# Expert rows of a routed mixture: weighted when they leave PSUM and added by indirect transfers onto a table of sums by token

## The chip, the cores and the metric

The kernel runs on one core of a Trainium2 chip. The metric is device time in microseconds (us) for one execution, as the median of several runs. All arithmetic is float32.

## The reference

One step of a hybrid decoder layer for 1,024 prompt tokens and 32 sample tokens (1,056 rows of 1,024 numbers). Three token mixers run side by side on a normalised input, their outputs pass one output projection, and the result is added to the input. Then each row is normalised again and goes through a hierarchical mixture of experts, and a last norm ends the step. The part that matters here:

```
def hier_moe(h, p):
    gl = h @ router_group_w + router_group_b          # 4 groups
    gsel = argmax(gl); gw = softmax(gl)[gsel]
    el = (h @ router_expert_w + router_expert_b)      # 16 experts, 4 in each group
    top_v, top_i = top_k(el[gsel], 2)
    tw = softmax(top_v) * gw
    gate = sum over the two choices of one_hot(gsel * 4 + top_i, 16) * tw
    for e in range(16):                               # SwiGLU of width 512
        he = silu(h @ w_gate[e]) * (h @ w_up[e])
        y = y + gate[e] * (he @ w_down[e])
    return y

x = x + mix                                           # residual after the mixers
x = x + hier_moe(rmsnorm(x, norm_ffn))
y_out = rmsnorm(x, norm_final)
```

## The kernel before, in words

The program is a sequence of blocks. The mixers take the first 830 us or so and are not touched. Three parts are touched.

**The output stage** (`output_stage`, from L1532). It projects the mixers' outputs tile by tile (nine tiles of 128 tokens, the last with 32), keeps the residual rows `x` in SBUF in `xy` (the tile "residual"), norms them and stores the normed rows in DRAM as `h2_rows` (L1621; the trace calls it h_rows). Between these stores the SyncE queue (SP) also stores zeros over the whole DRAM table `y_rows` (L1628; "expert_rows"), 5 transfers of 2,560 KB. At its end VectorE computes the routing (L2150 to L2237): the two experts of each token, their weights (`route.w`), and a packing of all (token, choice) pairs into slots. A slot is 32 rows of one expert; there are at most 96. `Bcol` is the one-hot of a pair's slot, `Arow` the one-hot of its place in the slot times an id, and 72 matmuls `Arow x Bcol` (L1925) give, for each slot, the ids of its 32 rows (`route.token`, "slot_rows"). The id is that of a quarter row: a row of 1,024 numbers is four quarters of 256, and a slot lies on the 128 partitions as 4 quarters by 32 rows. Places that no pair fills have the ids of the quarters of row 0. `route.slot` holds, the other way round, the place of each (token, choice) in `y_rows`.

**The experts** (`experts`, L2273). Every engine loops over the slots, q = 0, 1, ...; the loops over experts take their bounds from registers. In this run there are 74 slots, and GpSimd (POOL) and ScalarE (ACT), which loop in rounds of four slots, go through 76. For one slot:

- POOL waits until the gather of slot q has landed and until TensorE (PE) has read the previous slot, copies the ids of slot q + 3 (L2342) and the gathered rows (L2343, to `xg`, "slot_quarters"), drains, and issues the gather of slot q + 3 (L2329): 128 rows of 1 KB. Four buffers rotate.
- PE does the gate and up products of slot q (L2366), the down product of slot q - 1 (L2377), the transposes of slot q + 2 (L2359) and the transpose of the hidden rows of slot q (L2382).
- ACT applies silu (L2422), copies the finished rows out of PSUM into one of four buffers `y` ("slot_out", L2427), and stores them in order in `y_rows` (L2429), one row for each (token, choice).
- SP loads the weights of expert e + 3 as soon as PE has done with those of expert e: three buffers, 6 MB for an expert (gate and up at L2250 or L2266, down at L2270).

**The end** (`combine`, L2461). For each tile of tokens POOL gathers, from `y_rows`, the row of the first choice and the row of the second (L2478, 18 gathers of 512 KB, the last two of 128 KB). VectorE (DVE) multiplies each by its weight and adds it to the residual (L2509). ACT sums squares (L2497) and gets the scale with Ln and Exp (L2499, L2501), DVE scales by it and by norm_final (L2521), and SP stores the tile (L2487). Three pairs of buffers rotate.

## Time and profile before

| | us |
|---|---|
| median of 3 runs (1550.14 to 1559.4) | 1551.28 |
| the profiled execution, whole | 1556.24 |
| its span in the trace | 1554.5 |

| stretch of the span | us |
|---|---|
| output stage | about 835 to 1036 |
| experts | about 1036 to 1504 |
| end | about 1504 to 1554.5 |

The span is 1.74 us shorter than the profiled execution's own time, and that execution is 4.96 us longer than the median. In the tables of stretches a column gives how long each engine was busy; "PEclk" is the TensorE clock granted, as a share of full speed; "DMA share" is the mean busy share of the core's 16 DMA engines and GB/s what they moved. In rows of the timeline the first number is the start in us, the second how long the row lasted (or, for several instructions merged in one row, the time from the first to the last), and in brackets stands how long the engine was idle before and what ended it. "issue" is time in which the engine waited for nothing that the trace names.

### The profile page before, as it was taken

How to read it: one execution, taken by the hardware profiler on the slowest of the kernel's cores; microseconds unless marked ns; L12 is line 12 of the kernel's file. 1: busy time of each engine (PE TensorE's matmuls, PEld its weight loads, DVE VectorE, ACT ScalarE, POOL GpSimd, SP SyncE). 2: the span in 40 equal slices, each digit the busy share in tenths (PEclk: the TensorE clock that was granted, in tenths of full speed). 3: DMA queues.
4: the chain of work that ended last, by engine and by line, in shares of the span. 5: the costliest groups of instructions: out<-in, count | busy, mean ns of one | idle time of the engine just before them, and what ended most of it. 6: DMA issues, size and time to landing. Idle time of an engine off the chain costs nothing. (4 is left out here: it accounts for less than half of the span.)

```text
span 1554.5 us, 36931 instructions
## 1 busy us (share of the span) xinstructions
PE 1389.8 (89%) x15811; PEld 924.7 (59%) x15812; DVE 442.5 (28%) x1014; ACT 350.0 (23%) x823; POOL 362.4 (23%) x623
## 2 busy tenths in 40 slices
PE   7999999799999999999996999929999999999840
PEld 6666666466656988888883554425555555555520
DVE  3035533222222344444442112041111111111117
ACT  4012111232343233333321221200111111111113
POOL 8000000000003455455523021012222222222223
PEclk9999999899999799999998999959999999999985
DMA  5111111111101000000017434294555556999737
GB/s 170 27 42 37 33 41 27 27 28 41 28 19 28 2 9 9 9 9 9 9 52 251 172 155 149 66 357 165 203 209 206 201 215 215 332 375 317 262 124 260
DMA packets 118505, 190.12 MB, mean 122 GB/s; under 512 B 14496, under 2 KB 63127, under 8 KB 118410
## 3 DMA queue, kind: packets, MB, share of 16 engines
q1 hardware_dynamic: 100792, 159.30, 29.4%
q0 software_dynamic: 7392, 19.26, 3.7%
q10 hardware_dynamic: 10226, 10.19, 2.0%
q8 instruction: 73, 1.20, 0.3%
q14 instruction: 22, 0.18, 0.0%
HBM read 153.79 MB, written 34.92 MB: 121 GB/s over the span
## 5 line engine op out<-in xcount | busy, mean ns | idle before, releaser
L354 PE MATMUL ps<-hT,w_in 128*128 128x352 f32 (+1 forms) x1296 | 396.6, 465 | 0.8 <-DVE conv_state_T L702 0.8
L354 PEld LDWEIGHTS ps<-hT,w_in 128*128 128x128 f32 x1296 | 247.1, 191 | 140.5 <-issue 4.5
L2329 POOL DMA_INDIRECT gathered<-h_rows,gather_rows x79 | 76.4, 967 | 175.9 <-issue 167.7
L2366 PE MATMUL ps<-qkv,slot_T 128*32 128x256 f32 x1920 | 112.5, 387 | 4.3 <-issue 3.2
L2448 DVE TENSOR_TENSOR slot_T<-ps,vecs 128x256 f32<-128x256 f32 x75 | 31.8, 425 | 282.9 <-PE ps L2366 271.2
L2422 ACT ACTIVATE slot_silu<-ps 128x128 f32<-128x128 f32 x77 | 21.3, 277 | 307.0 <-PE ps L2366 299.1
L2366 PEld LDWEIGHTS ps<-qkv,slot_T 128*32 128x32 f32 x1920 | 60.7, 111 | 47.3 <-issue 11.5
L2366 PE MATMUL ps<-cb,slot_T 128*32 128x256 f32 x1408 | 80.5, 380 | 5.6 <-issue 5.6
L326 POOL DMA_DIRECT2D out_gdn_conv_prompt<-vbn x1 | 0.5, 518 | 297.2 <-ACT vbn L637 297.2
L1699 PE MATMUL ps<-qkv,zg 128*128 128x512 f32 (+1 forms) x144 | 66.2, 602 | 0.0
L2366 PEld LDWEIGHTS ps<-cb,slot_T 128*32 128x32 f32 x1408 | 43.9, 110 | 35.7 <-issue 9.6
L2377 PE MATMUL ps<-qkv,slot_hidden_T 128*32 128x256 f32 x960 | 57.4, 379 | 0.4 <-DVE slot_hidden_T L2458 0.4
L2427 ACT ACTIVATE slot_out<-ps 128x256 f32<-128x256 f32 x76 | 29.1, 383 | 104.6 <-PE ps L2377 104.6
L2458 DVE COPY slot_hidden_T<-ps 128x128 f32<-128x128 f32 x74 | 21.6, 292 | 108.1 <-PE ps L2382 108.1
L2342 POOL COPY gather_rows<-slot_rows 128x1 uint32 x76 | 14.3, 188 | 162.7 <-PE ps L2359 160.5
L778 DVE SCALAR_TENSOR_TENSOR zg<-pre,vecs,zg 128x1024 f32<-128x1024 f32 x36 | 46.2, 1284 | 3.5 <-issue 1.0
L2028 DVE TENSOR_TENSOR residual<-residual,ps 128x512 f32<-128x512 f32 (+1 forms) x18 | 12.3, 686 | 115.9 <-PE ps L1699 115.9
L2359 PE MATMUL ps<-ident,slot_quarters 128*128 128x128 f32 x152 | 33.5, 302 | 12.8 <-POOL slot_quarters L2343 12.8
L2377 PEld LDWEIGHTS ps<-qkv,slot_hidden_T 128*32 128x32 f32 x960 | 31.6, 110 | 20.6 <-issue 0.6
L1699 PEld LDWEIGHTS ps<-qkv,zg 128*128 128x128 f32 (+1 forms) x144 | 24.7, 181 | 30.1 <-issue 29.5
L2377 PE MATMUL ps<-third_w_down,slot_hidden_T 128*32 128x256 f32 x704 | 42.0, 379 | 0.0
L2377 PE MATMUL ps<-zg,slot_hidden_T 128*32 128x256 f32 x704 | 42.0, 379 | 0.0
(601 smaller groups left out, 2235.7 us busy)
## 6 DMA issues: line engine op xcount, KB each, us to landing
w_in<-in_w_in SPq DMA_DIRECT2D x28, 512.0 KB, 4.0
expert_rows<-zero_rows SPq DMA_DIRECT2D x5, 2560.0 KB, 9.4
qkv<-in_expert_w_gate SPq DMA_DIRECT2D x6, 2048.0 KB
qkv<-in_expert_w_up SPq DMA_DIRECT2D x6, 2048.0 KB
qkv<-in_expert_w_down SPq DMA_DIRECT2D x6, 2048.0 KB, 16.4
cb<-in_expert_w_gate SPq DMA_DIRECT2D x5, 2048.0 KB, 9.7
cb<-in_expert_w_up SPq DMA_DIRECT2D x5, 2048.0 KB, 16.7
zg<-in_expert_w_down SPq DMA_DIRECT2D x5, 2048.0 KB
```

Source lines behind the costliest of these rows:

```text
L354: last = pe.matmul(pbank(b)[:, c, 0:n], w[:, k, :], hT[:, k, c * CH:c * CH + n], start=(k == 0), stop=(k == KD - 1))
L778: dve.scalar_tensor_tensor(a_p, x_p, wv, a_p, ALU.mult, ALU.add)
L1699: last = pe.matmul(ps[0:n, half, :], mix[k][:, where(i)], wo[:, k, half * 512:half * 512 + 512], start=(k == 0), stop=(k == KD - 1))
L2329: pool.indirect_dma_start(ring[r][:], None, quarter_rows, bass.IndirectOffsetOnAxis(ap=idx[:, r:r + 1], axis=0)).then_inc(in_ring[r], 16)
L2342: pool.tensor_copy(idx[:, ahead:ahead + 1], route.token[:, ds(q + RING - 1, 1)])
L2359: last = pe.transpose(xT_bank[:, a * P:a * P + P], xg[:, a * P:a * P + P], m.ident[:])
L2366: last = pe.matmul(gu_bank[c4[c], 0:2 * QF].rearrange("p (x f) -> p x f", x=2), xT[:, k % 2, k // 2, :], by_block[u][k][:, :, c * QF:c * Q ...
L2377: last = pe.matmul(y_bank[c4[c], 0:QD], heT[:, c4[k]], wd[u][:, k, c * QD:c * QD + QD], start=(k == 0), stop=(k == 3))
L2422: act.activation(sl[:], gu_bank[:, 0:QF], ACT.Silu).then_inc(s.silu, 1)
L2427: act.activation(y[r][:], y_bank[:, 0:QD], ACT.Copy).then_inc(s.acc, 1)
L2448: dve.tensor_tensor(xT[:], xT_bank[:, 0:2 * P].rearrange("p (s c t) -> p s c t", s=2, c=4), bc(nf, 3, ROWS_SLOT), ALU.mult).then_inc(s.xT, 1)
L2458: dve.tensor_copy(heT[:], hT_bank[:, 0:QF]).then_inc(s.hT, 1)
```

## The change

- Two DRAM tables get 32 spare rows. `y_rows`, its zeros and `route.slot` go. Instead SP stores each residual tile in a table `sum_rows` right after the store of its normed rows, and zeros in the spare rows of both tables.
- Places of a slot that no pair fills now have the ids of spare rows, each its own, so that the 128 ids of a slot all differ. For this the ids are computed as an offset from the spare rows (a few more DVE operations at the start of the output stage, `behind`).
- A second product of 72 matmuls, at the start of the expert block, gives the weight of each place of each slot (`route.weight`); `Arow` is multiplied by the choice weights for it. DVE copies it out before the first slot.
- ACT scales a slot's rows by these weights when it copies them out of PSUM, and no longer issues a store.
- POOL issues, one slot after the other, an indirect transfer that adds the 128 quarter rows onto `sum_rows`. Before each it waits until the previous one has landed (`out_y[(r - 1) % RING]`), since two slots may hold the same token. The gather comes without a drain now. In the loop POOL does `next_rows(q + 4)` (the old work, for slot q + 4) and then `add_rows(q)`.
- The end loads the nine tiles of `sum_rows` in order on SP, ACT does the sums of squares (Ln and Exp once for two tiles), DVE one scaling, and SP stores.

```diff
@@ output_stage, SP @@
                 def out_rows(i):
                     sp.wait_ge(s.h2, i + 1)
                     sp.dma_start(h2_rows[where(i), :], h2[i % 2][0:rows(i), :]).then_inc((s.h2o0, s.h2o1)[i % 2], 16)
-
-                blank = y_rows.rearrange("(z p a) d -> z p a d", z=5, p=P)
+                    sp.dma_start(sum_rows[where(i), :], x_tile(i)).then_inc(s.xo, 16)
+
                 for i in range(6):
                     out_rows(i)
-                    if i < 5:
+                    if i == 0:
                         sp.wait_ge(s.zeros, 1)
-                        sp.dma_start(blank[i], bc(zeros[:], 1, ROUNDS * RING * ROWS_SLOT // (5 * P))).then_inc(s.zf, 16)
+                        for spare_of in (h2_rows, sum_rows):
+                            sp.dma_start(spare_of[NTOK:NTOK + ROWS_SLOT, :], xy[NS:2 * NS, NT, :]).then_inc(s.xo, 16)
@@ output_stage, DVE, routing @@
                 for c, w in enumerate((w1, w2)):
-                    dve.tensor_copy(route.w[:, c, :], w[:].rearrange("p t o -> p (t o)"))
+                    dve.tensor_copy(route.w[:, c, 0:NT], w[:, 0:NT, 0])
+                    dve.tensor_tensor(route.w[:, c, NT:TILES], w[:, NT, :], valid[:], ALU.mult)
...
                 for c in range(2):
-                    last = dve.tensor_tensor(by_choice[:, c], by_choice[:, c], bc(ids[:], 2, ROWS_SLOT), ALU.mult)
+                    last = dve.tensor_tensor(by_id[:, c], by_choice[:, c], behind[:], ALU.mult)
                 last.then_inc(s.rt, 1)
-
-                dve.scalar_tensor_tensor(rk[:], fk[:], float(ROWS_SLOT), rk[:], ALU.mult, ALU.add)
+                dve.drain()
+                for c in range(2):
+                    dve.tensor_tensor(by_choice[:, c], by_choice[:, c], bc(route.w[:, c, :], 2, ROWS_SLOT), ALU.mult)
@@ experts, POOL @@
-                pool.tensor_copy(idx[:, 0:RING - 1], route.token[:, 0:RING - 1])
+                def next_rows(q, r, loads, copies):
+
+                    pool.wait_ge(in_ring[r], 16 * loads)
+                    pool.wait_ge(s.xTp, q + 1)
+                    if copies is not None:
+                        pool.wait_ge(s.xg, q)
+                        pool.wait_ge(s.ix, copies)
+                    pool.tensor_copy(idx[:, r:r + 1], route.token[:, ds(q + RING, 1)]).then_inc(s.ix, 1)
+                    pool.tensor_copy(xg[:], ring[r][:]).then_inc(s.xg, 1)
+                    gather((r + RING - 1) % RING)
+
+                def add_rows(q, r, stored, copies):
+
+                    pool.wait_ge(s.acc, q + 2)
+                    if stored is not None:
+                        pool.wait_ge(out_y[(r - 1) % RING], 16 * stored)
+                    pool.wait_ge(s.ix, copies)
+                    pool.tensor_copy(sidx[:, (r + 1) % RING:(r + 1) % RING + 1], route.token[:, ds(q + 1, 1)]).then_inc(s.ix, 1)
+                    pool.indirect_dma_start(quarter_sums, bass.IndirectOffsetOnAxis(ap=sidx[:, r:r + 1], axis=0), y[r][:], None,
+                                            compute_op=ALU.add).then_inc(out_y[r], 16)
...
-                n = rounds(pool)
-                with pool.Fori(0, n) as i:
+                m = more_rounds(pool)
+                for r in range(RING):
+                    next_rows(r, r, 1, r if r else None)
+                for r in range(RING):
+                    next_rows(r + RING, r, 2, RING + 2 * r)
+                    add_rows(r, r, 1 if r else None, RING + 2 * r + 1)
+                with pool.Fori(1, m) as i:
                     for r in range(RING):
-                        q, ahead = RING * i + r, (r + RING - 1) % RING
-                        pool.wait_ge(in_ring[r], 16 * (i + 1))
-                        pool.wait_ge(s.xTp, q + 1)
-                        pool.tensor_copy(idx[:, ahead:ahead + 1], route.token[:, ds(q + RING - 1, 1)])
-                        pool.tensor_copy(xg[:], ring[r][:]).then_inc(s.xg, 1)
-                        pool.drain()
-                        gather(ahead)
+                        q = RING * i + r
+                        next_rows(q + RING, r, i + 2, RING + 2 * q)
+                        add_rows(q, r, i + 1 if r else i, RING + 2 * q + 1)
+                for r in range(RING):
+                    q = RING * m + r
+                    add_rows(q, r, m + 1 if r else m, RING + 2 * RING * m + r)
@@ experts, PE @@
+                for a in range(2 * TILES):
+                    for c in range(4):
+                        last = pe.matmul(ps[c4[c], 7, 0:TABLE], row_weights[:, a, :], slot_onehot[:, a, :], start=(a == 0), stop=(a == 2 * TILES - 1))
+                last.then_inc(s.wt, 1)
@@ experts, ACT @@
-                    act.activation(y[r][:], y_bank[:, 0:QD], ACT.Copy).then_inc(s.acc, 1)
-                    act.wait_ge(s.acc, q + 2)
-                    act.dma_start(y_rows[ds(q * ROWS_SLOT, ROWS_SLOT), :].rearrange("t (c f) -> c t f", c=4), y[r][:]).then_inc(out_y[r], 16)
+                    act.activation(y[r][:], y_bank[:, 0:QD], ACT.Copy, scale=route.weight[:, ds(q, 1)]).then_inc(s.acc, 1)
@@ combine, SP @@
-                sp.dma_start(wrow, A["norm_final"].partition_broadcast(P)).then_inc(s.w, 16)
+                for t in range(TILES):
+                    sp.dma_start(x[t][0:n[t]], sum_rows[t * P:t * P + n[t], :]).then_inc(x_in[t], 16)
+                    if t == 1:
+                        sp.dma_start(wrow, A["norm_final"].partition_broadcast(P)).then_inc(s.w, 16)
```

On POOL, one slot of the expert loop (the last of a round of four) stood so before; "gathered" are the four ring buffers, "slot_quarters" is `xg`, and the rows ISA are waits.

```order
L2342 ISA
L2342 COPY gather_rows<-slot_rows 128x1
L2343 COPY slot_quarters<-gathered 128x256
L2329 DMA gathered<-h_rows,gather_rows 128x256
L2337 REGISTER_ALU
L2337 COMPARE_AND_BRANCH
```

The same slot now:

```order
L2359 ISA
L2360 ISA
L2360 COPY gather_rows<-slot_rows 128x1
L2361 COPY slot_quarters<-gathered 128x256
L2350 DMA gathered<-h_rows,gather_rows 128x256
L2369 REGISTER_ALU
L2370 ISA
L2370 COPY scatter_rows<-slot_rows 128x1
L2371 DMA sum_rows<-slot_out,scatter_rows 4352x256
L2385 REGISTER_ALU
L2385 COMPARE_AND_BRANCH
```

The adding transfer (L2371) and its copy of ids now stand on POOL behind the gather of each slot, with waits ahead of the copy. The store of a slot has left ACT's queue.

On SP, from the end of the expert block to the end of the program, there stood:

```order
L2294 UNCONDITIONAL_BRANCH
L2481 UNCONDITIONAL_BRANCH
L2483 DMA qkv<-in_norm_final 128x1024
L2487 DMA out_y_prompt<-residual 128x1024 x8
L2487 DMA out_y_sample<-residual 32x1024
```

And now:

```order
L2311 UNCONDITIONAL_BRANCH
L2527 UNCONDITIONAL_BRANCH
L2530 DMA qkv<-sum_rows 128x1024 x2
L2532 DMA qkv<-in_norm_final 128x1024
L2530 DMA qkv<-sum_rows 128x1024 x6
L2530 DMA qkv<-sum_rows 32x1024
L2536 DMA out_y_prompt<-qkv 128x1024 x8
L2536 DMA out_y_sample<-qkv 32x1024
```

Nine loads now stand ahead of the nine stores on the same queue, and the 18 gathers on POOL are gone.

## Rows read from the trace of the kernel before

**Rows 1.** Stretches: us, busy time of each engine with instructions, clock, DMA share, GB/s.

```profile
1020.00:1035.00 15.00, 5.65 (x144) 5.30 (x148) 8.69 (x30) 0.00 (x0) 0.00 (x0) 0.55 1.04 392
...
1200.00:1300.00 100.00, 98.06 (x1675) 56.51 (x1671) 15.35 (x51) 11.02 (x34) 26.22 (x52) 1.00 0.56 204
...
1440.00:1460.00 20.00, 17.89 (x309) 10.26 (x305) 2.73 (x9) 1.98 (x6) 3.91 (x9) 1.00 1.03 382
1475.00:1500.00 25.00, 21.06 (x356) 11.96 (x348) 3.46 (x12) 3.91 (x14) 5.43 (x10) 1.00 0.17 51
1520.00:1540.00 20.00, 0.00 (x0) 0.00 (x0) 16.84 (x14) 6.91 (x17) 11.33 (x9) 0.50 0.99 364
```

**Rows 2.** Timeline of PE: the gate and up products of two slots in a row.

```profile
1190.28 3.66 PE L2366 MATMUL ps<-qkv,slot_T 128*32 128x256 f32 x64
...
1196.07 3.66 PE L2366 MATMUL ps<-qkv,slot_T 128*32 128x256 f32 x64
```

**Rows 3.** Waits of PE in the expert stage: us in total, times, longest.

```profile
PE ps L2359 <- POOL slot_quarters L2343: 12.8, 8, 8.0
```

**Rows 4.** Timeline of POOL, gathers back to back and then with PE as the slower.

```profile
1068.13 0.97 POOL L2329 DMA_INDIRECT gathered<-h_rows,gather_rows  x1 [2.08 <-issue]
...
1069.23 0.40 POOL L2343 COPY slot_quarters<-gathered 128x256 f32<-128x256 f32 x1
1071.65 0.97 POOL L2329 DMA_INDIRECT gathered<-h_rows,gather_rows  x1 [2.02 <-issue]
...
1220.81 0.96 POOL L2329 DMA_INDIRECT gathered<-h_rows,gather_rows  x1 [0.84 <-issue]
```

**Rows 5.** The same: first and last of 12 gathers issued with POOL never free.

```profile
1398.90 0.97 POOL L2329 DMA_INDIRECT gathered<-h_rows,gather_rows  x1 [5.10 <-issue]
...
1473.32 0.97 POOL L2329 DMA_INDIRECT gathered<-h_rows,gather_rows  x1 [4.44 <-issue]
```

**Rows 6.** The gather's line over the whole span: landing, counted from the issue's start.

```profile
DMA to landing us min/median/max: 2.7/5.4/7.2
```

**Rows 7.** Timeline of PE: first slots of two experts with three slots each.

```profile
1411.64 3.66 PE L2366 MATMUL ps<-qkv,slot_T 128*32 128x256 f32 x64 [0.48 <-issue]
1430.85 3.66 PE L2366 MATMUL ps<-cb,slot_T 128*32 128x256 f32 x64 [1.75 <-issue]
```

**Rows 8.** DMA issues by line: KB each, median us to landing.

```profile
qkv<-in_expert_w_gate SPq DMA_DIRECT2D x6, 2048.0 KB
...
out_y_sample<-residual SPq DMA_DIRECT2D x1, 128.0 KB, 2.0
```

**Rows 9.** Timeline of the routing, the second product's model, and of the first gather.

```profile
1018.42 0.24 DVE L2188 COPY choice_weights<-r_w 128x9 f32<-128x9 f32 x2
...
1029.63 0.82 DVE L2225 TENSOR_TENSOR ub<-ub,quarter_rows 128x288 f32<-128x288 f32 x2 [0.43 <-issue]
...
1030.51 4.80 PE L1925 MATMUL ps<-bb,ub 128*32 128x104 f32 x144 [9.35 <-DVE ub L2225]
...
1037.06 1.11 POOL L2329 DMA_INDIRECT gathered<-h_rows,gather_rows  x1 [0.88 <-issue]
...
1042.74 0.18 POOL L2342 COPY gather_rows<-slot_rows 128x1 uint32 x1 [2.05 <-DMA gathered<-h_rows,gather_rows]
```

**Rows 10.** Timeline of the end: last evictions and stores, first and last instructions.

```profile
1496.97 0.38 ACT L2427 ACTIVATE slot_out<-ps 128x256 f32<-128x256 f32 x1
...
1500.28 0.55 ACTq L2429 DMA_DIRECT2D expert_rows<-slot_out  x1
1504.21 0.34 SPq L2483 DMA_DIRECT2D qkv<-in_norm_final  x1
...
1552.13 0.34 SPq L2487 DMA_DIRECT2D out_y_sample<-residual  x1
```

**Rows 11.** Queues and groups of the end alone (1504 to 1554.5): packets, MB, share.

```profile
q0 software_dynamic: 2400, 8.65, 49.4%
q1 hardware_dynamic: 1344, 4.85, 25.2%
```

More of the change, by code:

```diff
@@ L58 @@
 gb gcum kd gl gcT gcs gco bk zt zte""".split()
-MOE_SEMS = "g0 g1 g2 d0 d1 d2 r0 r1 r2 r3 ix xg xTp xT gu silu he hTp hT down acc y0 y1 y2 y3".split()
-FIN_SEMS = "w c0 c1 c2 used rstd y out".split()
+MOE_SEMS = "g0 g1 g2 d0 d1 d2 r0 r1 r2 r3 wt wtd ix xg xTp xT gu silu he hTp hT down acc y0 y1 y2 y3".split()
+FIN_SEMS = "w x0 x1 x2 x3 x4 x5 x6 x7 x8 ones rstd y out".split()
 ROWS_SLOT, SLOTS, RING = 32, 96, 4
@@ L2492, in _ @@
                 act.preload_act_table_set(LNEXP)
-                for t in range(TILES):
-                    n = P if t < NT else NS
-                    act.drain()
-                    act.wait_ge(s.used, t + 1)
-                    act.activation(junk[0:n], xy[0:n, t, :], ACT.Square, accum_out=ssq[0:n, t, 0:1])
-                    act.drain()
-                    act.activation(ssq[0:n, t, 1:2], ssq[0:n, t, 0:1], ACT.Ln, scale=1.0 / D, bias=NORM_EPS)
-                    act.drain()
-                    act.activation(ssq[0:n, t, 0:1], ssq[0:n, t, 1:2], ACT.Exp, scale=-0.5).then_inc(s.rstd, 1)
+                act.wait_ge(s.ones, 1)
@@ new lines, in _ @@
+                for a, b in groups:
+                    for t in range(a, b):
+                        act.wait_ge(x_in[t], 16)
+                        act.activation(junk[0:n[t]], x[t][0:n[t]], ACT.Square, accum_out=ssq[0:n[t], 0, t:t + 1])
+                        act.drain()
+                    act.activation(ssq[:, 1, a:b], ssq[:, 0, a:b], ACT.Ln, scale=1.0 / D, bias=NORM_EPS)
+                    act.drain()
+                    act.activation(ssq[:, 0, a:b], ssq[:, 1, a:b], ACT.Exp, scale=-0.5).then_inc(s.rstd, 1)
@@ L2503, in _ @@
             @block.vector
             def _(dve):
-                def add(t):
-                    n = P if t < NT else NS
-                    dve.wait_ge(got[t % 3], 32 * (t // 3 + 1))
-                    for c in range(2):
-                        last = dve.scalar_tensor_tensor(xy[0:n, t, :], rows[t % 3][c][0:n], route.w[0:n, c, t:t + 1], xy[0:n, t, :], ALU.mult, ALU.add)
-                        if c == 0:
-                            dve.drain()
-                    last.then_inc(s.used, 1)
+                dve.memset(ssq[:], 1.0).then_inc(s.ones, 1)
```

127 lines of the change are left out of this document (69 added, 58 removed).

## The prediction

> **What bounds the kernel now.** I read the stretches first, then the timelines of PE and POOL in the expert stage, then the timeline of the end. From 1100 to 1475 PE is busy almost throughout; between 1200 and 1300 it is 98.06 of 100 us [rows 1]. One slot takes 1196.07 - 1190.28 = 5.79 us of PE [rows 2], and 74 of them are 428 of the stage's 468 us, which also hold its first gathers and its last stores. So the expert stage is bound by PE, and a term that lengthens POOL's work costs nothing until POOL needs more than 5.79 us for a slot.
>
> POOL is near that point. A gather lands 2.7 us after its issue starts at best, 5.4 in the median and 7.2 at worst [rows 6]. Where POOL is behind, the next gather starts 1071.65 - 1068.13 = 3.52 us after the last, and the copies between them end 2.0 us before it; where PE is the slower, the gap ahead of the gather is 0.84 [rows 4]. 2.7 + 0.84 = 3.54: I read this as the drain, which holds POOL until the previous gather has landed. Under heavy weight traffic the same distance is (1473.32 - 1398.90) / 11 = 6.77 us [rows 5], so a gather lands there in 6.77 - 0.84 = 5.9 us. This is over 5.79: in that stretch POOL sets the pace, and PE waits for its copies; over the whole stage these waits are 12.8 us in 8 places, 8.0 of them before the first slot [rows 3].
>
> From 1497.35, when the last real slot has been evicted, to 1554.5 is a tail of 57.2 us [rows 10]. In it the DMA engines are the bound: 0.99 busy at 364 GB/s from 1520 to 1540 [rows 1], with 8.65 MB gathered and 4.85 MB on the other queue (norm_final and the stores) [rows 11].
>
> **Part 1, the output stage.** The zeros (5 x 2,560 KB) go and 4.3 MB of residual rows come; both lie beside 150 us of PE work, and no PE wait names them: 0. The routing chain at its end is exposed. The weights take four instructions for two: +0.2 (two last 0.24 [rows 9]). The multiplication that forms the ids keeps its size. Multiplying `Arow` by the weights costs 0.8 us (as L2225, 0.82) and lies beside the 4.8 us of the first product [rows 9]. Sum +0.3; bounds 0 and +1.5. The second product is another 4.8 us of PE, from about 1036.3; the first gathered rows are there only at 1042.74 [rows 9], so it is covered with over a microsecond to spare, and 0 is taken; without that cover it would cost at most 4.8.
>
> **Part 2, the expert stage.** Removed: the store on ACT, which nothing waits for, and the drain on POOL. Its best gain is what PE waits for POOL after the first slot, 12.8 - 8.0 = 4.8 us. Added: one indirect transfer for each slot, in a chain. Each waits for the one before to land, then comes a copy of ids (0.19) and a gap like those before an issue (0.3) and the semaphore (about 0.15): period = landing + 0.65. Behind the waiting transfer stands the work for the next slot's rows, and PE waits for that.
>
> The landing of a transfer that adds onto DRAM is in no row. The nearest is the gather, the same 128 rows of 1 KB on the same queue. Quiet, I take 3.5 us (2.7, and 0.8 for a read of the table ahead of the write); its period is then 4.15, under 5.79, and free. Under load the low bound is the gather's 5.9. The high bound is 9.1: the gather's loaded part, 5.9 - 2.7 = 3.2, paid twice. I take 7.5, the middle, since the nearest row is 5.9 and there are a read more and a gather just ahead in the same queue. The loaded period is 8.15.
>
> An expert's weights are three times 2,048 KB [rows 8], 6.29 MB, at 375 GB/s (between 364 and 392 [rows 1]) 16.8 us. In the experts of five to eight slots the loaded 16.8 us see two chain steps, which put POOL behind by 2 x (8.15 - 5.79) = 4.7 us; POOL may lag about 5 to 7 us before PE misses its rows (with PE as the slower it copies them most of a slot ahead of their use), and then catches up at 4.15. Cost 0. The experts of three slots are another matter: from 1411.64 to 1430.85 one took 19.2 us [rows 7]. With the chain: 16.8 / 8.15 = 2.06 slots while loaded, 0.94 x 4.15 = 3.9 us for the rest, 20.7 us in all, +1.5. There are seven such from 1357 on: +10.5, less 4.5 of the lag that is allowed and not used up before: **+6**. With 5.9: period 6.55, 2.56 slots, 1.8 us for the rest, 18.6: no loss, and up to 4.8 gained. With 9.1: period 9.75, 1.72 slots, 5.3, 22.1 us: +2.9 x 7 = **+20**.
>
> The Trainium skill has a rule that speaks against this part. "Collectives: The Full Stack", section "The bandwidth ceiling", says of adding in the DMA path that it is slow not for the add but for its two source reads on one ring, and gives a ratio of 1.93 for throughput. No row here shows an adding transfer. By that rule the loaded landing would be at the 9.1 end, a rival below.
>
> **Part 3, the tail.** Before: 57.2 us. Now, from 1497.35: slots 74, 75 and 76 (the last two of them empty) are added in a chain. 0.5 to the first issue, 3 x 3.5 + 2 x 0.65 = 11.8 to the last landing. Before, from the last store's issue at 1500.28 to SP's first instruction at 1504.21 were 3.9 us [rows 10]; with 2.0 for the landing of 128 KB [rows 8], 1.9 are left for the change of blocks. So the end begins at 1497.35 + 0.5 + 11.8 + 1.9 = 1511.6, 7.3 later than before. Its traffic: 4.33 MB of sums and 0.52 MB of norm_final in, 4.33 MB out, 9.2 MB against 13.5, at 375 GB/s 24.5 us, with 1.5 to the first byte and 1.0 after the last: 27. DVE, busy 16.84 of 20 us there with three operations for a tile [rows 1], has one left, and ACT was busy 6.91; both lie beside the transfers. End at 1538.6: **-16**. Bounds: scatters at 2.7 and 392 GB/s give -20, scatters at 6 and 364 give -8.
>
> **Sum.** 0.3 + 6 - 16 = -9.7 on the span: 1544.8, the profiled execution 1546.5, and on the median, which lies 4.96 below that of the profiled execution, 1551.3 - 9.7 = 1541.6. About 1%, some 15.5 us, is what a measurement of this kernel can tell from no change.
>
> **Rivals.**
> - *The adding is as cheap as the gather.* Loaded landing 5.9 and quiet 2.7 to 3. The removed drain speaks for it, and that one queue (ACT's stores) no longer competes. Expert stage -3 to 0, tail -17 to -20: -19, 1532. Against it: there is a read that a gather has not.
> - *Two reads count twice.* Loaded landing 9.1: +20 - 16 + 0.3 = +4, 1555. For it: the stretch from 1399 to 1473 shows POOL already over PE's pace at 5.9. Beside this stands the skill's rule above.
> - *The chain overtakes PE (slower).* The place is the wait before each adding transfer. It decides from a quiet landing of 5.79 - 0.65 = 5.1 us, since then every slot and not only the loaded ones pays. At a quiet landing of 6.0 each of 74 slots costs 0.86 more, 64, less 7 of lag; the tail gives only -8: +49, 1600. At 3.5 quiet and 10.5 loaded (period 11.15: 1.5 slots, 6.2 us, 23 us per expert) it is +27 there and some +8 in the longer experts, so +19, 1570. For it: each step reads, adds and writes DRAM and waits for the receipt, and under load plain gathers take up to 7.2 already [rows 6]. Against it: quiet, 128 KB goes to DRAM in 2.0 us [rows 8], and the gather in 2.7.
>
> **How the numbers follow.** Forecast (landing 6.5 to 8.5 under load, -16 to -2): 0.43, of which 0.12 faster by over 1% and 0.31 within. As cheap as the gather: 0.22, faster. Counted twice: 0.14, within 1%. Chain overtakes PE: 0.21, slower. That is faster 0.34, within 0.45, slower 0.21. The forecast's own range is 1535 to 1550. The range asked for reaches to the cheap case with its best tail, -23 or 1528, and over the two-reads case into the lower half of the slow one, 1578; about 0.1 is left above and 0.07 below.
>
> **What would show it.** The landing of the adding transfer, quiet and loaded: 3.5 and 7.5. POOL's waits before the copy of its ids: none where the DMA share is about 0.5, some between 1350 and 1475. The gap ahead of a gather shrinks to about 0.3 under load. PE's waits for slot_quarters rise from 12.8 to about 20 us. Slots in quiet stretches still take 5.79. Three adding transfers in a row after PE's last product, and then 27 us to the end with DMA at 0.95 or more. I am wrong if quiet slots get longer than 5.79, if SP starts its loads much earlier or later than 14 us after the last real eviction, or if the end block takes far from 27 us.

## The result, and the profile after

| | us |
|---|---|
| before, median of 4 runs (1549.28 to 1559.4) | 1550.71 |
| changed, median of 4 runs (1572.52 to 1575.22) | 1574.06 |
| ratio | 1.0141, 95% interval 1.0107 to 1.0174 |
| span of the profiled execution, before and after | 1554.5 and 1571.8 |

The change makes the kernel slower by 1.4%. 1541.6 was forecast. 1574.06 lies outside the forecast's own range (1535 to 1550) and on the wrong side of no change; it is inside the wider one (1528 to 1578) only because that reaches into the slow rival. One execution of the kernel before, measured beside e10 and e11, took 4,994 us and is left out of their intervals. The spans differ by 17.3 us, and they divide so (each time is the start of an eviction on ACT; before has its first at 1059.02 and the last real one at [rows 10]):

| part | before | after | difference |
|---|---|---|---|
| start of the span to the first eviction | 1059.02 | 1057.36 | -1.7 |
| first to last real eviction, 73 slots on | 437.95 | 467.87 | +29.9 |
| last real eviction to the end | 57.5 | 46.6 | -10.9 |

Two stretches before, and then those of the changed kernel, with the columns of [rows 1]:

```profile
1300.00:1400.00 100.00, 96.11 (x1639) 55.50 (x1635) 15.47 (x51) 11.23 (x34) 23.90 (x49) 1.00 0.87 320
1400.00:1500.00 100.00, 89.02 (x1513) 51.28 (x1505) 13.64 (x45) 11.44 (x36) 22.24 (x45) 1.00 0.66 234
```

```profile
1200.00:1300.00 100.00, 95.19 (x1619) 54.81 (x1612) 14.86 (x49) 12.51 (x33) 55.04 (x84) 1.00 0.66 193
1300.00:1400.00 100.00, 86.94 (x1426) 49.38 (x1422) 12.74 (x42) 10.53 (x28) 46.67 (x70) 0.97 0.91 306
1400.00:1500.00 100.00, 84.31 (x1378) 47.93 (x1374) 12.74 (x42) 10.53 (x28) 50.23 (x77) 0.97 0.76 250
...
1560.00:1570.00 10.00, 0.00 (x0) 0.00 (x0) 5.92 (x5) 3.71 (x10) 0.00 (x0) 0.50 1.00 408
```

Two things stand there. In the stretches with the most weight traffic PE is busy 87 and 84 us of 100, where before it was 96 and 89 (the latter with 3 us after its last eviction); and the granted clock is 0.97 in two stretches in which it was 1.00 before. The clock has two levels, full and half, so a mean of 0.97 over 100 us is 6 us at half clock, and work worth 3 us at full clock is not done in them.

The waits from 1055 to 1500, of POOL and then of PE:

```profile
POOL scatter_rows L2370 <- DMA sum_rows<-slot_out,scatter_rows: 149.4, 61, 5.7
```

```profile
PE ps L2412 <- POOL slot_quarters L2361: 20.7, 16, 2.6
PE ps L2419 <- issue: 15.2, 15, 1.9
```

L2370 is the copy of ids ahead of the adding transfer (L2371), so the first row is the wait for the previous slot's transfer, 61 times for the 69 transfers of this stretch, 149.4 us in all. In the same stretch before, PE waited 3.5 us for POOL's copies and 12.4 on "issue" (the rest of the 12.8 of [rows 3] came ahead of it).

POOL's timeline, two steps under weight traffic and then quiet ones:

```profile
1183.46 1.60 POOL L2371 DMA_INDIRECT sum_rows<-slot_out,scatter_rows  x1 [0.51 <-issue]
1184.49 0.77 POOL L2360 COPY gather_rows<-slot_rows 128x1 uint32 x1
1184.62 0.98 POOL L2361 COPY slot_quarters<-gathered 128x256 f32<-128x256 f32 x1
1185.77 1.01 POOL L2350 DMA_INDIRECT gathered<-h_rows,gather_rows  x1 [0.17 <-issue]
1191.39 0.18 POOL L2370 COPY scatter_rows<-slot_rows 128x1 uint32 x1 [4.61 <-DMA sum_rows<-slot_out,scatter_rows]
1192.08 1.60 POOL L2371 DMA_INDIRECT sum_rows<-slot_out,scatter_rows  x1 [0.50 <-issue]
...
1203.41 1.60 POOL L2371 DMA_INDIRECT sum_rows<-slot_out,scatter_rows  x1 [0.50 <-issue]
...
1207.51 0.18 POOL L2370 COPY scatter_rows<-slot_rows 128x1 uint32 x1 [0.78 <-DMA sum_rows<-slot_out,scatter_rows]
1208.20 1.60 POOL L2371 DMA_INDIRECT sum_rows<-slot_out,scatter_rows  x1 [0.51 <-issue]
```

Read it as a chain. The transfer issued at 1183.46 lets the next copy of ids go at 1191.39: it landed after 7.93 us, and the step to the next issue is 1192.08 - 1183.46 = 8.62 us. Quiet, the landing is 1207.51 - 1203.41 = 4.10 and the step 4.79. A step is the landing and 0.69 us. The issue lasts 1.60 us, where a gather's lasts 0.97 [rows 4], and POOL's copies right behind it last 0.77 and 0.98 instead of 0.18 and 0.40; the gaps ahead of the gathers from 1060 to 1500 are 0.16 to 0.27, so the hold in [rows 5], up to 6.5 us there, is gone with the drain.

What late rows do to PE, two slots of its timeline:

```profile
1374.84 1.91 PE L2430 MATMUL ps<-qkv,slot_hidden_T 128*32 128x256 f32 x32
1378.93 0.43 PE L2412 MATMUL ps<-ident,slot_quarters 128*128 128x128 f32 x2 [2.18 <-POOL slot_quarters L2361]
...
1379.41 5.35 PE L2419 MATMUL ps<-qkv,slot_T 128*32 128x256 f32 x64
...
1387.47 0.43 PE L2412 MATMUL ps<-ident,slot_quarters 128*128 128x128 f32 x2 [0.99 <-POOL slot_quarters L2361]
...
1389.87 5.28 PE L2419 MATMUL ps<-cb,slot_T 128*32 128x256 f32 x64 [1.86 <-issue]
```

The granted clock in two stretches of 5 us inside it (columns: length, PE busy, clock, DMA share, GB/s):

```profile
1380.00:1385.00 5.00, 5.00 (x68) 0.70 1.07 374
...
1390.00:1395.00 5.00, 5.00 (x68) 0.68 1.07 369
```

The waits are paid twice: 2.18 us idle before the transposes at 1378.93, and then a gate and up product of 5.35 us instead of 3.66, because part of it ran at 1.2 GHz. Not every wait has this effect: after those of 2.15 and 2.56 us that ended at 1274.78 and 1312.86 the clock stayed at 1.00.

The end of the stage, in order of time:

```profile
1524.50 1.59 POOL L2371 DMA_INDIRECT sum_rows<-slot_out,scatter_rows  x1 [1.39 <-issue]
...
1525.23 0.47 ACT L2481 ACTIVATE slot_out<-ps,slot_weights 128x256 f32<-128x256 f32 x1
...
1529.25 1.57 POOL L2371 DMA_INDIRECT sum_rows<-slot_out,scatter_rows  x1 [0.47 <-issue]
...
1533.82 1.57 POOL L2371 DMA_INDIRECT sum_rows<-slot_out,scatter_rows  x1 [0.47 <-issue]
1537.91 0.18 POOL L2370 COPY scatter_rows<-slot_rows 128x1 uint32 x1 [2.53 <-DMA sum_rows<-slot_out,scatter_rows]
1538.57 1.57 POOL L2371 DMA_INDIRECT sum_rows<-slot_out,scatter_rows  x1 [0.47 <-issue]
1545.31 0.81 SPq L2530 DMA_DIRECT2D qkv<-sum_rows  x2
```

Four transfers in a row, 4.6 to 4.75 us apart, and SP's first load 19.6 us after the last real eviction has ended. From there to 1571.8 are 26.5 us, where 27 were predicted.

Where the 29.9 us of the stage are: the slots need 432 us when nothing waits (the experiments below). In the changed kernel PE waits 20.7 us for POOL's copies, "issue" is 4.6 more than in e5, which has no such waits (15.2 against 10.6), and PE is busy 10.0 us longer than in e5 (430.7 against 420.7) for the same products: 6 to 7 of these are half clock, and 2 are a stretched down product in the first five and the last slots (below). That is 35.3 of the 35.7 us above 432. Before stood 6 above 432. Of the 20.7 us, 7.2 fall in the long experts ahead of 1357 and 13.5 in the experts of three slots after it.

### The profile page after: what moved, and what is told of

It reads as the page before. It is cut to its first block and busy times, and to the rows that moved or that the text cites. A ratio compares the mean times of both kernels' runs of the same rounds, so it can differ in the third digit from the quotient of the medians.

```text
span 1571.8 us, 37521 instructions
## 1 busy us (share of the span) xinstructions
PE 1402.1 (89%) x15955; PEld 932.1 (59%) x15956; DVE 421.6 (27%) x1006; ACT 355.1 (23%) x815; POOL 480.1 (31%) x757
## 5 line engine op out<-in xcount | busy, mean ns | idle before, releaser
L2371 POOL DMA_INDIRECT sum_rows<-slot_out,scatter_rows x76 | 121.9, 1604 | 36.7 <-issue 28.6
L2419 PEld LDWEIGHTS ps<-qkv,slot_T 128*32 128x32 f32 x1920 | 61.6, 112 | 49.5 <-issue 14.4
L2350 POOL DMA_INDIRECT gathered<-h_rows,gather_rows x79 | 79.7, 1009 | 14.6 <-issue 13.9
L2419 PEld LDWEIGHTS ps<-cb,slot_T 128*32 128x32 f32 x1408 | 45.0, 113 | 38.7 <-issue 14.0
L2370 POOL COPY scatter_rows<-slot_rows 128x1 uint32 (+1 forms) x76 | 14.0, 185 | 159.9 <-DMA sum_rows<-slot_out,scatter_rows 156.8
L2481 ACT ACTIVATE slot_out<-ps,slot_weights 128x256 f32<-128x256 f32 x76 | 36.1, 475 | 114.7 <-PE ps L2430 114.7
L2361 POOL COPY slot_quarters<-gathered 128x256 f32<-128x256 f32 x76 | 61.5, 809 | 0.2 <-issue 0.2
L2360 POOL COPY gather_rows<-slot_rows 128x1 uint32 (+1 forms) x76 | 45.3, 596 | 38.6 <-issue 19.1
L2412 PEld LDWEIGHTS ps<-ident,slot_quarters 128*128 128x128 f32 x152 | 15.4, 141 | 55.3 <-issue 52.3
```

What stands on the lines that cost most here:

```text
L2350: pool.indirect_dma_start(ring[r][:], None, quarter_rows, bass.IndirectOffsetOnAxis(ap=idx[:, r:r + 1], axis=0)).then_inc(in_ring[r], 16)
L2360: pool.tensor_copy(idx[:, r:r + 1], route.token[:, ds(q + RING, 1)]).then_inc(s.ix, 1)
L2361: pool.tensor_copy(xg[:], ring[r][:]).then_inc(s.xg, 1)
L2371: pool.indirect_dma_start(quarter_sums, bass.IndirectOffsetOnAxis(ap=sidx[:, r:r + 1], axis=0), y[r][:], None, compute_op=ALU.add).then_in ...
L2412: last = pe.transpose(xT_bank[:, a * P:a * P + P], xg[:, a * P:a * P + P], m.ident[:])
L2419: last = pe.matmul(gu_bank[c4[c], 0:2 * QF].rearrange("p (x f) -> p x f", x=2), xT[:, k % 2, k // 2, :], by_block[u][k][:, :, c * QF:c * Q ...
```

## The experiments

All but e3 and e9, which start from the kernel before, are edits of the changed kernel; the diffs show the lines that matter. "Stage" is from the first to the last real eviction, "tail" from the start of the latter to the end of the span. Spans and waits are of one profiled execution each; PE's waits are those for POOL's copies of gathered rows in the stage, without what comes ahead of the first eviction. Some kernels leave work out: e4 the adding transfers, e1 the sums (a row holds its last writer's values), e2 and e12 three of the four tables at the end, and e8, e14 and e9 the loads of the weights of experts 3 to 15.

| kernel | time, us | runs | span | stage | PE waits | tail |
|---|---|---|---|---|---|---|
| before | 1550.71 | 4 | 1554.5 | 438.0 | 3.5 | 57.5 |
| changed | 1574.06 | 4 | 1571.8 | 467.9 | 20.7 | 46.6 |
| changed again (e15) | 1576.93 | 1 | 1575.2 | 466.9 | 19.0 | 45.8 |
| no adding transfers (e4) | 1529.56 | 1 | 1527.8 | 430.9 | 0 | 35.2 |
| two tables, wait two back (e5) | 1541.28 | 4 | 1539.4 | 432.2 | 0 | 49.4 |
| the same again (e13) | 1551.7 | 1 | 1550.0 | 432.2 | 0 | 49.5 |
| two tables, wait one back (e11) | 1588.96 | 4 | 1588.7 | 466.8 | 20.4 | 57.1 |
| groups interleaved, wait three back (e6) | 1533.96 | 4 | 1535.5 | 431.6 | 0 | 37.6 |
| groups interleaved, wait one back (e10) | 1577.21 | 4 | 1575.9 | 472.2 | 23.7 | 45.3 |
| plain writes in the chain (e1) | 1555.87 | 1 | 1553.9 | 446.5 | 0.7 | 40.8 |
| four tables (e2) | 1561.29 | 1 | 1558.8 | 453.7 | 0 | 37.6 |
| the same again (e12) | 1537.24 | 1 | 1535.5 | 432.2 | 0 | 37.4 |
| changed, no weight traffic (e8) | 1558.24 | 1 | 1555.6 | 452.4 | 0 | 46.1 |
| the same again (e14) | 1536.66 | 1 | 1534.9 | 431.3 | 0 | 46.1 |
| before, no weight traffic (e9) | 1557.67 | 1 | 1555.9 | 432.7 | 1.6 | 55.3 |
| before without the drain (e3) | 1550.3 | 10 | 1546.7 | 432.4 | 0 | 55.9 |

### The wait alone, with two tables

```
-    pool.indirect_dma_start(quarter_sums, ...
+    pool.indirect_dma_start(tables[r % 2], ...
e5 alone:
-    pool.wait_ge(out_y[(r - 1) % RING], 16 * stored)
+    pool.wait_ge(out_y[(r - 2) % RING], 16 * stored)
```

The second table starts from zeros; the end loads both, and DVE adds them (these edits, the same in e5 and e11, are not shown).

Expected of e5: 

> The changed kernel with two tables (even slots onto the residual rows, odd slots onto zeros), each with its own chain, so a step has two slots' time; the end loads both and adds them. Theory: loaded landing 8.6 + 0.7 is under 2 x 5.79, so the expert stage is back at its old length, 28 us shorter than in the changed kernel, and the adding transfers after the last slot overlap in pairs, 6 to 8 us less; the end has 4.3 MB more to load, 11 us more. Sum -25: about 1548 to 1552 against 1550.7 before and 1574 changed. Rivals A and B: the stage keeps its length and the end is longer: 1580 or more.

Expected of e11: 

> The kernel with two tables of sums (even slots on one, odd slots on the other, both read and added at the end), with the wait for the slot before put back, though the two write to different tables. Theory (the wait is the cost, not two transfers that meet in one table): the expert stage is as long as in the changed kernel (468 us from the first to the last eviction, against 432 with the wait for two back) and the time some 33 to 38 above that of the two tables, 1574 to 1580. Rival (the cost is contention for one table's rows): within 5 us of the kernel with two tables, 1541 to 1546.

Expected of e13, the kernel of e5 beside e11: 

> The kernel with two tables and the wait for two back, once more, beside the four tables on one chip. If the slots of 6.11 us belong to the program of the four tables: 1538 to 1545 with slots at 5.79. If they belong to the chip: as the four tables beside it, plus or minus 5.

e5 takes 1541.28 us, 0.9907 of before (0.9878 to 0.9935), below the 1548 to 1552 that I had expected. e11 takes 1588.96, 1.0221 of the before on its chip (1.017 to 1.0272). The two differ only in which transfer is waited for: the stage goes from 432.2 to 466.8 us and the tail grows by 8. Against e13, on e11's chip, the spans differ by 38.7. The chain is the cost, not two transfers that meet in one table: in e11 neighbours go to different tables and the loss is whole. The time I had expected for e11 (1574 to 1580) was too low because it took e5's run as the base: e13 came out 10 us above e5, with the first eviction at 1068.31 instead of 1057.81 and the same stage. That offset arises ahead of the experts: the routing's product (L1934) starts at 1028.99 in e5 and at 1039.77 in e13. Its cause is open. The times of before spread as widely, from 1547.9 to 1561.6, but whether for the same reason is not shown.

### The order of the experts

e6 takes the experts in the order 0, 4, 8, 12, 1, 5, ... Both experts of a token are of one group, so the two rows of a token then lie at least seven slots apart, and a transfer need only wait for that of three slots back. Each of four neighbouring slots has its own spare rows for empty places. The diff shows the order and the wait; the ids of the spare rows and the unrolled loop on SP are left out.

```
-    sel[:, c].rearrange("p t (g e) -> p t g e", e=EPG)
+    sel[:, c].rearrange("p t (e g) -> p t e g", g=NG)
-    load(3 * i + u, u, bound(sp, 3 * i + u - 2))
+    load((j % NG) * EPG + j // NG, j % 3, bound(sp, j - 2))
e6 alone:
-    pool.wait_ge(out_y[(r - 1) % RING], 16 * stored)
+    pool.wait_ge(out_y[(r - 3) % RING], 16 * stored3)
```

Expected of e6: 

> The changed kernel with the experts in an order in which four neighbours belong to four groups (0, 4, 8, 12, 1, 5, ...). Both experts of a token are of one group and each expert has at least two slots, so slots of one token are at least seven apart; each transfer waits only for the one three slots back. Four sets of spare rows; some 2.5 us more of routing on DVE. One table, the end as in the changed kernel. Theory: expert stage as before or 3 us shorter, adding transfers after the last slot overlap (7 us less), end 26.5 us: 1550.7 - 1.4 + 2.5 - 3 - 18 = about 1531, between 1526 and 1537. Rival A or B: 1560 or more.

Expected of e10: 

> The kernel of the interleaved groups of experts, with the wait of the changed kernel put back: each adding transfer waits for that of the slot before. Same order of the weights, same spare rows, same 76 transfers. Theory (the wait makes POOL late, and what counts is how many steps of the chain fall on weight traffic and whether POOL's lead of 4.6 us is refilled between them): 13 loads of 16.8 us at 8.6 a step are 25 loaded steps, 25 x (8.6 - 5.79) = 71 us of delay, against 49 quiet steps that give back up to 1.0 each: the expert stage comes to 25 x 8.6 + 49 x 4.8 = 450 us at best against 431 of PE alone, and with three steps of tail the time is 1556 to 1572. Rival 1 (the order of the experts brought the gain and the wait costs nothing): 1534, as with the wait for three back. Rival 2 (the order does nothing for the chain): 1574 as the changed kernel.

e6 takes 1533.96 us, 0.9853 of before (0.9816 to 0.9891): the fastest of those that compute everything. It has the same 76 issues of 1.6 us, one table and the end of the changed kernel. PE's only wait for POOL from 1055 to 1500 in e6 ends at 1059.70, ahead of the first eviction at 1066.33:

```profile
PE ps L2430 <- POOL slot_quarters L2379: 0.8, 1, 0.8
```

e10 takes 1577.21, 1.0166 of before (1.0107 to 1.0225), with these waits and, in its first stretches, this clock:

```profile
PE ps L2430 <- POOL slot_quarters L2379: 23.7, 12, 3.6
```

```profile
1100.00:1200.00 100.00, 87.70 (x1413) 49.52 (x1414) 13.02 (x43) 10.89 (x29) 48.57 (x74) 0.95 0.76 250
1200.00:1300.00 100.00, 89.19 (x1477) 50.58 (x1469) 13.56 (x45) 11.26 (x30) 47.16 (x71) 0.97 0.86 287
```

So the order by itself brings nothing, and the second rival of e10 stands. My 450 us for its stage was a best case, in which no quiet step is wasted on a POOL that is already ahead, and it left out the clock, which over e10's stage (0.95, 0.97, 0.98 and 0.97 in four stretches of 100 us) took 13 us. In numbers: 431.6 of e6, 23.7 of waits, 13 of clock and 3.6 more "issue" (13.6 against 10.0) make 471.9, against 472.2 measured.

After the last eviction e6 needs less as well, since its last transfers do not wait for each other:

```profile
1499.29 1.57 POOL L2389 DMA_INDIRECT sum_rows<-slot_out,scatter_rows  x1 [0.27 <-POOL scatter_rows L2388]
...
1501.23 1.57 POOL L2389 DMA_INDIRECT sum_rows<-slot_out,scatter_rows  x1 [0.16 <-POOL scatter_rows L2388]
...
1503.17 1.57 POOL L2389 DMA_INDIRECT sum_rows<-slot_out,scatter_rows  x1 [0.16 <-DMA sum_rows<-slot_out,scatter_rows]
1509.98 0.81 SPq L2548 DMA_DIRECT2D qkv<-sum_rows  x2
```

They are 1.94 us apart instead of 4.6 to 4.75, and the tail is 37.6 us instead of 46.6.

The Trainium skill, "DMA: Bandwidth & Descriptors", section "Rules for kernel authors", has the rule behind the wait: an accumulating DMA reads its destination and writes it later, and nothing holds the bytes in between, so another access of the same bytes must wait for its semaphore. The rule speaks of the same bytes. No run here breaks it, so none shows what that would do. e5 and e6 keep it and are fast; what cost the time was to apply it to neighbouring slots whose bytes could have been kept apart.

### No transfers, plain transfers, four tables

```
e4:  -    pool.indirect_dma_start(quarter_sums, ..., compute_op=ALU.add).then_inc(out_y[r], 16)
     +    pool.sem_inc(out_y[r], 16)
e1:  -    compute_op=ALU.add
e2:  -    pool.wait_ge(out_y[(r - 1) % RING], 16 * stored)
     +    pool.wait_ge(out_y[(r - 3) % RING], 16 * stored3)
     -    pool.indirect_dma_start(quarter_sums, ...
     +    pool.indirect_dma_start(tables[r], ...
```

Expected of e4: 

> The changed kernel without the adding transfers (the experts' results are left out; POOL keeps the waits for the evictions and the copies of ids). It gives the stage with neither chain, nor issues, nor their traffic. Theory: last real eviction 1492 to 1496, and four tables (which has issues and traffic but no chain) within 2 us of this. If four tables is much later than this, the issues or the traffic cost something by themselves.

Expected of e1: 

> The changed kernel, with the transfers to the table of sums as plain writes (no add; so the sums are left out and a row holds its last writer's values). The chain of waits stays. Last real eviction: 1497.35 us before, 1525.70 in the changed kernel. Theory (a chain whose step is the landing of the adding transfer, 4.1 us quiet and 8 to 8.6 under weight traffic, plus 0.7): the read is a part of that landing, so quiet landing about 3 us, loaded about 6, last real eviction near 1500. Rival A (POOL's own instructions, 1.6 us for the issue of an adding transfer, make POOL too slow): the issue falls to about 1.0 us as for the gather, and the eviction comes near 1500 too, but with the landing unchanged. Rival B (the adding transfers take DMA bandwidth from the weights): near 1515, with the landing as it was.

Expected of e2: 

> The changed kernel with four tables of sums, one for each of the four buffers, so that a transfer waits only for the one three slots back; the same 76 adding transfers, each with its read and 1.6 us of issue. The end reads only the first table, so three quarters of the sums are left out. Theory: without the chain the last real eviction is back at 1494 to 1498 (28 us earlier than in the changed kernel), and PE waits for slot_quarters under 5 us. Rival A (POOL's issues): stays at 1520 or later. Rival B (bandwidth): stays at 1515 or later, with PE waiting for weights between 1350 and 1480.

Expected of e12, the kernel of e2 beside e13: 

> The kernel with four tables once more, beside the two tables on one chip. In its first run nothing waited and yet each slot took 6.11 us in place of 5.79: the 32 matmuls of the down product took 2.2 to 2.3 us instead of 1.91. The changed kernel shows the same in its first five and last five slots, where POOL is not late. If this belongs to the program: 1559 to 1562 again, slots at 6.11, while the two tables run at 5.79 beside it. If it belongs to the chip of that batch: both kernels here alike, either 1540 to 1545 or 1562 to 1566.

e4 has the floor: a stage of 430.9 us. e6 does all its transfers in 431.6, e5 and e12 in 432.2. So with the wait out of the way the 1.6 us that POOL spends on each issue and the traffic cost at most 1.3 us together.

e1 keeps the chain but its transfers land sooner. POOL's timeline under weight traffic, and in the tail:

```profile
1423.94 1.01 POOL L2371 DMA_INDIRECT sum_rows<-slot_out,scatter_rows  x1 [0.51 <-issue]
...
1429.90 0.18 POOL L2370 COPY scatter_rows<-slot_rows 128x1 uint32 x1 [3.27 <-DMA sum_rows<-slot_out,scatter_rows]
```

```profile
1514.61 0.98 POOL L2371 DMA_INDIRECT sum_rows<-slot_out,scatter_rows  x1 [0.48 <-issue]
1517.34 0.18 POOL L2370 COPY scatter_rows<-slot_rows 128x1 uint32 x1 [1.75 <-DMA sum_rows<-slot_out,scatter_rows]
```

A plain transfer lands in 5.96 us under traffic and 2.73 quiet, where an adding one takes 7.93 and 4.1; its issue lasts 1.0 instead of 1.6. PE's waits for POOL are 0.7 us, although the wait for the slot before is still there. How much of this the shorter landing does is not shown by itself, since many slots of e1 took 6.11 us (below), which gives the chain more time. The first queue's packets, adding and then plain:

```profile
q0 software_dynamic: 15936, 20.57, 7.0%
```

```profile
q0 software_dynamic: 8640, 20.57, 3.8%
```

7,296 packets more for 76 transfers is 96 more for each, for the same bytes.

The stages of e1, e2 and e8 were nevertheless 16 to 23 us above the floor, with next to no wait in the profile, and the last real evictions came later than I had expected. Nearly all slots of e2 and e8, and many of e1, took about 6.11 us and not 5.79; e1's down products change between 1.91 and 2.2 to 2.3 us within the one execution. The down product of one slot on PE, in e2 and then in e12, a later run of the same kernel:

```profile
1207.91 2.21 PE L2434 MATMUL ps<-qkv,slot_hidden_T 128*32 128x256 f32 x32
```

```profile
1205.35 1.91 PE L2434 MATMUL ps<-qkv,slot_hidden_T 128*32 128x256 f32 x32
```

At a granted clock of 1.00 in both, these 32 matmuls last 2.2 to 2.3 us in nearly all slots of e2, and 1.91 in all of e12. e12 ran at 1537.24 with a stage of 432.2, 24 us under e2. So the stretched product belongs to an execution, or to part of one, and not to the program (the first case of my expectation for e12 falls; the second too, as e9 and e2 shared a chip and only e2 had it). All four executions that show it carry these indirect writes: e1, e2, e8 and, in its first five and last slots only, the profiled one of the changed kernel; but most executions with such writes do not show it. What causes it stays open.

### Without the weight traffic

```
-    load_gate_up(...), load_down(...)        of experts 3 to 15
+    sp.sem_inc(in_gu[u], 16 * loads_gu[u])
+    sp.sem_inc(in_d[u], 16)
```

Expected of e8, on the changed kernel: 

> The changed kernel without the weight loads of experts 3 to 15 (their arithmetic runs on the weights of experts 0 to 2; the loads are left out). Theory: all landings are quiet, a step of the chain takes 4.7 to 4.8 us, under the 5.79 of PE, and the last real eviction comes within 3 us of that of the old kernel treated in the same way. Rival A (POOL's issues): it comes about 25 us later than there. Rival B: within 3 us too.

Expected of e9, the same edit on before: 

> The kernel before without the weight loads of experts 3 to 15 (left out in the same way). It is the measure for the changed kernel so treated. Gathers land in 2.7 us throughout, slots take 5.79 us, so from the first slot (1044.4) 74 slots and 16 starts of experts at about 0.5: last real eviction near 1483 to 1490. All theories.

Expected of e14, the kernel of e8 again: 

> The changed kernel without the weight loads of experts 3 to 15 (their results are computed with the weights of the first three), once more. Theory (the chain costs nothing where its step of 4.1 + 0.7 us is under the 5.79 us of a slot, the whole loss comes from steps under weight traffic): slots at 5.79 unless the down product is stretched again, no wait of PE for POOL's copies, 432 us from the first to the last real eviction, and 46 from there to the end with its four transfers in a row: a time of 1537 to 1548. Rival (POOL's own longer work, 1.6 us to issue an adding transfer beside 1.0 for a gather, costs too): over 440 us in the stage, with waits of PE for POOL's copies.

Expected of e15, the changed kernel beside e14: 

> The changed kernel itself, beside the one without weight traffic on one chip. By the theory 465 to 470 us from the first to the last real eviction, of which some 20 us are PE's waits for POOL's copies and 5 to 15 are half-clock stretches that follow them, and a time of 1570 to 1590. The rival gives the two kernels of this batch the same stage within 5 us.

e8 alone could not be read, for its slots of 6.11 us. e9 says that before hardly depends on the traffic: its stage is 432.7 us against 438.0 (its time is no lower because its first eviction came at 1067.94, with the late start seen above). e14 can be read. Two steps of the chain on POOL, in e14:

```profile
1201.26 1.61 POOL L2375 DMA_INDIRECT sum_rows<-slot_out,scatter_rows  x1 [0.16 <-issue]
1204.90 0.18 POOL L2364 COPY gather_rows<-slot_rows 128x1 uint32 x1 [2.03 <-PE ps L2416]
...
1206.98 1.61 POOL L2375 DMA_INDIRECT sum_rows<-slot_out,scatter_rows  x1 [0.17 <-issue]
```

Here the chain of 4.8 us runs inside a slot of 5.79, and it is POOL that waits for PE. The stage is 431.3 us, with no wait of PE for POOL and a clock of 1.00 to the last product. e15 on the same chip has 466.9, 19.0 us of such waits, and these stretches:

```profile
1200.00:1300.00 100.00, 95.72 (x1608) 54.83 (x1604) 14.54 (x48) 12.03 (x32) 56.76 (x85) 0.98 0.60 177
1300.00:1400.00 100.00, 87.13 (x1442) 49.82 (x1438) 13.15 (x44) 10.80 (x29) 46.74 (x70) 0.97 0.92 310
1400.00:1500.00 100.00, 86.84 (x1374) 48.40 (x1369) 12.31 (x42) 10.25 (x27) 47.71 (x73) 0.93 0.80 260
```

Means of 0.98, 0.97 and 0.93 are 12 us lost to half clock. 19.0 + 12 + 5.1 more "issue" (14.8 against 9.7) is 36.1, for a difference of 35.5. The whole loss of the stage comes from steps of the chain under weight traffic. The tails of e14 and e15 are the same (46.1 and 45.8): there the chain costs its four steps with or without weights.

### Before without the drain

The second experiment on the kernel before, with `pool.drain()` replaced by a semaphore that the copy of ids increments; the ids are copied one slot earlier.

Expected: 

> The kernel before, with its gathers issued without the drain (ids copied one round earlier, semaphores in its place). My reading of the drain: it holds POOL until the previous gather has landed. If so, the gap ahead of a gather is 0.2 to 0.3 us also under weight traffic (before 0.84 quiet and 4.4 to 6.5 loaded), the 12 gathers from 1399 on are spaced as PE's slots, PE's 4.8 us of waits for slot_quarters after the first slot go, and the time falls by 3 to 6 us. If the gap is something else of the indirect issue (room in its ring), it stays and the time is the same.

Ten runs give 0.9982 of before (0.9959 to 1.0004): no change that can be told. In the profile the gaps ahead of the gathers are 0.18 to 0.29 us but for one of 0.52, where before they went up to 6.5, so the drain did hold POOL. PE's waits for POOL go from 3.5 us to none and the stage from 438.0 to 432.4, 5.6 us. That is near the most I had put on it, 4.8 us, but the times don't show it.

## Why the prediction was wrong

**What held.** PE bounds the stage until POOL needs more than 5.79 us for a slot; e4, e5, e6, e12 and e14 all have slots of 5.79. The second product was covered: the ids behind the first gathered rows were copied at 1041.31, where before it was 1042.74 [rows 9], 1.4 us earlier, for a forecast of 0.3 later. This is no measured gain: the first eviction of the same changed kernel came 5.2 us later in e15. The end's traffic took 26.5 us for 27. The chain of waits on POOL was the mechanism, and e5 against e11 shows it. The drain did hold POOL, as e3 shows.

**The step that failed: "Part 2", and in it "Cost 0" for the experts of five to eight slots, and the sum of +6.** The stage became 29.9 us longer. Three of its sizes were off, all to the same side.

- The quiet step: 4.15 predicted (3.5 + 0.65), 4.79 measured (4.10 + 0.69). The 0.8 us that I put on the read of the table stood in no row; against the plain transfer's 2.73 the adding one takes 1.4 more. So a late POOL regains 5.79 - 4.79 = 1.0 us a slot and not 1.64.
- The loaded step: 8.15 predicted, 8.62 measured in the row above, and a load of weights at times touches a third step. The transfers issued at 1126.58, 1135.88 and 1143.84 land after 8.61, 7.28 and 6.91 us; with 0.69 each and less 5.79 they make POOL 3.5 + 2.2 + 1.8 = 7.5 us late. The next three loads, read in the same way, make it 5.7, 6.3 and 6.0. I had 4.7.
- The lead: I let POOL "lag about 5 to 7 us before PE misses its rows". In e5 the copy of a slot's rows ends 4.6 us ahead of its transposes, slot after slot; in the changed kernel this lead falls from 5.1 to 0.1 us in one load of weights and comes back by 1.0 a slot, and in an expert with few slots it is never whole when the next load starts. From 1362 to 1478 it is never above 0.83, and mostly near 0.1.

Put into the method of "Part 2", an expert of three slots has 16.8 / 8.62 = 1.95 slots under load and 1.05 x 4.79 = 5.0 us for the rest, 21.8 us instead of 19.2, which is +2.6, seven times +18. Less the 4.5 us of lag that "Part 2" allowed, this is 13.7, and PE waited 13.5 us after 1357. The other 7.2 us of waits fell in the longer experts, where I had put 0. Against before the account of the stage closes so: 17.2 us more waits for POOL, 2.8 more "issue" (15.2 against 12.4) and 9.5 more busy time (430.7 against 421.2) are 29.5 of the 29.9.

**The term that was missing: the clock.** No case of mine held it. Idle stretches of PE of 1.4 us ahead of 1370.89 and 2.2 us ahead of 1378.93 were followed by half clock. This took 6 us in the changed kernel's profile, beside 20.7 us of waits; in e15 it was 12 beside 19.0, and in e10 13 beside 23.7.

**The tail.** -16 predicted, -10.9 measured. The end of the last real eviction to SP's first load is 19.6 us and not 14.2: the chain holds four transfers and not three, since that of the slot before had only just been issued when the last real slot was evicted, and each step is 4.6 to 4.75 instead of 4.15. This was a sign that I had named (SP starting much later than 14 us after the last real eviction). Of the 27 us to the end, the 1.5 to the first byte and the 1.0 after the last stood in no row; the sum came out at 26.5, but its parts are not shown.

**The rivals.** "Two reads count twice" gave +20 for the stage; it was near the 20.7 us of waits by luck: it had the loaded landing at 9.1, where 7.93 is typical and 8.98 the longest, and took off none of the lag that the forecast allowed. The slow rival named the right place, but neither of its conditions came: a quiet landing over 5.1 us (4.1 measured), or one of 10.5 under load. Its second case, 1570, is the closest number to 1574.06, and this too is luck, as the clock is not in it. The rule of the Trainium skill in "Collectives: The Full Stack", section "The bandwidth ceiling", points the right way: adding costs more than moving. Its ratio of 1.93 is one of throughput; for the landing of this transfer the rows show 4.1 against 2.73 quiet, 1.5, and 7.93 against 5.96 under load, 1.3. The cheap case, 5.9 and 2.7 to 3, is what a plain transfer does.

## What to carry to other kernels

A wait of each step for the landing of the one before turns a latency into a rate. In this kernel the step was 4.79 us quiet and 8.62 under load, with 5.79 us of PE work beside it. Price it at the landing under the heaviest traffic, not at its average, and ask how large the lead of the waiting engine is and how fast it is refilled: a chain can fit on average and still be late in every burst.

Order only what touches the same bytes. If the work can be arranged so that neighbours never share them (another order of the experts, one more table), the same transfers cost next to nothing (431.6 us in e6, 430.9 without them in e4). And when PE is made to wait, put the half clock that can follow on the bill.

## What the hardware showed that was not expected

- An indirect transfer that adds onto DRAM holds POOL 1.60 us at its issue, against 1.0 for a plain one, and two small copies behind it then last 0.77 and 0.98 us instead of 0.18 and 0.40. It takes 96 packets more for the same 128 KB.
- Short waits can be followed by half clock on PE: in the changed kernel no idle time was longer than 2.56 us, in slots of 5.79 us of work, and the clock still fell four times between 1377 and 1463.
- The same program can run its down product in 1.91 us or in 2.2 to 2.3, at the same granted clock, for nearly a whole execution (e2 against e12, e8 against e14: 24 and 22 us). Read alone, e2 would have put this on the transfers.
